# A two-block model in one program: weights and inputs as on-chip images, one weight ring, layers written out, small stages folded away

## What is computed

```python
# first block, per layer l of 2
h = rms_norm(x, attn_norm_g[l])
pa, pb, pc = split(h @ w_in[l], (1056, 768, 448))
x = x + concat([rwkv7_mixer(pa, ...), dilated_mixer(pb, ...), mla_mixer(pc, ...)]) @ w_out[l]
h = rms_norm(x, ffn_norm_g[l])
x = x + (silu(h @ w_gate[l]) * (h @ w_up[l])) @ w_down[l]          # d_ff = 2816
x = rms_norm(x, final_norm_g)                                       # after both layers
# second block, per layer i of 2; a second stream xc (256 context tokens) starts from ctx
mod  = silu(c) @ ada_w[i] + ada_b[i];  modc = silu(c_ctx) @ ada_w[i] + ada_b[i]
h, hc = modulate(rms_norm(x)), modulate(rms_norm(xc))
q, k, v = project_qkv(h);  qc, kc, vc = project_qkv(hc)
x = x + g1 * (attention(q, [kc, k], [vc, v]) @ w_o[i])              # global in layer 0, window in layer 1
x = x + g2 * peer_ffn(modulate(rms_norm(x)))                        # xc likewise, in layer 0 only
# peer_ffn: 8 heads x 16 experts of 16384 per token, u and v rows of 1024 floats gathered per expert
```

## Time and profile before

| | |
|---|---|
| median of 3 runs | 3671.6 us (3670.44 to 3678.66) |
| the profiled execution | 3673.66 us, span 3671.7 us |
| granted TensorE clock, mean | 0.907 of full speed |
| PE busy | 2794.8 us (76% of the span) |
| DVE busy | 2234.2 us (61%) |
| ACT busy | 594.1 us (16%) |
| POOL busy | 1167.0 us (32%) |
| moved by DMA | 1030.17 MB, mean 281 GB/s |

### The profile page before, as it was taken

One profiled execution on the slowest core, in us unless ns is written; L12 is line 12 of the kernel. 1 busy time (PEld: TensorE's weight loads), 2 busy tenths in 40 slices (PEclk: granted clock), 3 DMA queues, 4 the chain that ended last, 5 costly groups with the idle time before them and its releaser, 6 DMA issues. The chain is left out here.

```text
span 3671.7 us, 31943 instructions
## 1 busy us (share of the span) xinstructions
PE 2794.8 (76%) x10155; PEld 1786.7 (49%) x10155; DVE 2234.2 (61%) x5260; ACT 594.1 (16%) x1616; POOL 1167.0 (32%) x1028
## 2 busy tenths in 40 slices
PE   7884568689958777998688577777759857777776
PEld 1573445478846455886457233232227743233222
DVE  0339666666556757565577777565536277776554
ACT  1221120120001102000131111111112211111111
POOL 0000244334434432445131444444400014444442
PEclk9997789789979868999899799999979989999999
DMA  8420677559978755898553899999941239999997
GB/s 285 158 90 12 240 255 271 183 196 356 364 272 311 256 175 191 309 360 308 212 180 141 342 420 421 421 421 421 416 158 69 71 127 420 421 420 420 420 419 291
DMA packets 279599, 1030.17 MB, mean 281 GB/s; under 512 B 23498, under 2 KB 74728, under 8 KB 213504
## 3 DMA queue, kind: packets, MB, share of 16 engines
q0 software_dynamic: 147456, 805.37, 56.2%
q1 hardware_dynamic: 130464, 219.82, 17.1%
q10 hardware_dynamic: 1504, 2.87, 0.2%
HBM read 1022.16 MB, written 5.82 MB: 280 GB/s over the span
## 5 line engine op out<-in xcount | busy, mean ns | idle before, releaser
L2217 PE MATMUL ps<-w_ring,diag 128*128 128x512 f32 x1216 | 576.7, 621 | 172.9 <-ACT diag L2197 172.9
L1308 POOL DMA_INDIRECT ctx_ring<-in_peer_u,expert_now x256 | 308.9, 1207 | 928.4 <-DVE expert_now L494 415.9
L2217 PE MATMUL ps<-own,diag 128*128 128x512 f32 x832 | 406.4, 636 | 204.4 <-ACT diag L2197 204.4
L2131 DVE SCALAR_TENSOR_TENSOR w_ring<-w_ring,htok 128x1024 f32<-128x1024 f32 x304 | 372.2, 1224 | 242.1 <-DMA w_ring<-in_peer_uv,expert 241.6
L2217 PEld LDWEIGHTS ps<-w_ring,diag 128*128 128x128 f32 x1216 | 227.3, 195 | 518.5 <-ACT diag L2197 280.3
L2118 POOL DMA_INDIRECT w_ring<-in_peer_uv,expert x304 | 336.5, 1107 | 404.1 <-PE ps L2217 391.4
L2118 POOL DMA_INDIRECT own<-in_peer_uv,expert x208 | 221.7, 1066 | 705.6 <-POOLq L161 396.5
L1320 DVE SCALAR_TENSOR_TENSOR ctx_ring<-ctx_ring,h_now 128x1024 f32<-128x1024 f32 x256 | 306.7, 1224 | 120.4 <-DMA ctx_ring<-in_peer_u,expert_now 110.5
L2217 PEld LDWEIGHTS ps<-own,diag 128*128 128x128 f32 x832 | 159.8, 201 | 448.2 <-ACT diag L2197 277.3
L2131 DVE SCALAR_TENSOR_TENSOR own<-own,htok 128x1024 f32<-128x1024 f32 x208 | 254.6, 1224 | 185.8 <-DMA own<-in_peer_uv,expert 185.6
L1324 DVE SCALAR_TENSOR_TENSOR ctx_sum<-ctx_ring,weight_now,ctx_sum 128x1024 f32<-128x1024 f32 x208 | 267.0, 1284 | 126.7 <-DMA ctx_ring<-in_peer_v,expert_now 118.5
(11 more groups left out here) (419 smaller groups left out, 3774.5 us busy)
## 6 DMA issues: line engine op xcount, KB each, us to landing
w_ring<-in_ada_w SPq DMA_DIRECT2D x24, 2048.0 KB
w_ring<-in_peer_w_q SPq DMA_DIRECT2D x12, 2048.0 KB
w_ring<-in_ffn_w_gate SPq DMA_DIRECT2D x22, 1024.0 KB
w_ring<-in_ffn_w_up SPq DMA_DIRECT2D x22, 1024.0 KB
w_ring<-in_ffn_w_down SPq DMA_DIRECT2D x10, 2048.0 KB
w_ring<-in_w_qkv SPq DMA_DIRECT2D x9, 2048.0 KB
w_ring<-in_w_o SPq DMA_DIRECT2D x6, 2048.0 KB
w_ring<-in_w_in SPq DMA_DIRECT2D x6, 2048.0 KB
```

The source lines that it names most:

```text
L1308: pool.indirect_dma_start(out=m.ctx_ring[:, r % CTX_RING, :], out_offset=None, in_=expert_tables(self.d)[r // SLOTS], in_offset=bass.Indir ...
L2131: v.scalar_tensor_tensor(out=u, in0=u, scalar=1.0, in1=m.htok[:, blk, :], op0=ALU.mult, op1=ALU.mult, accum_out=b.dots[:, e:e + 1]).then_i ...
L2217: ins = pe.matmul(m.ps[:, 2 * blk + half, :], b.diag[:, e % DIAGS, :], entry(e)[:, D + half * 512:D + (half + 1) * 512], start=(k == 0), s ...
```

## The change

- Weights: the host writes each weight group as the image of its slot, `[128, n]`, one behind the other, so each load is one DMA with one contiguous run per partition (16 KB for most). One ring counts through the whole program. `peer_queries` of the context stream, and each `feed_forward`, now load the next stage's first three groups.
- Vectors, x, ctx, the peer keys and the lora matrices come from the host as they lie on the chip; the transposes for them go. The output is written feature by token and turned by the host.
- `load_constants`, both `load_inputs`, `context_keys`, `context_back` and `second_modulation` go. Their loads and the rotary angles move into `modulation`, the latent tables and keys into the second `feed_forward`, and the rest into layer 0's `peer_experts`, before expert 16 on PE and before expert 18 on VectorE.
- The first block's layers are written out; the copies at the start of `in_projection` go, and POOL's gathers no longer wait for them. The expert sums of the context stream stay on the chip.
- `peer_experts` keeps ten entries: three of its own, one in `hT`, six in the weight ring; its accumulator's copy moves into `hT`.

```diff
@@ WeightRing
-            for dst, src in self.groups[g](layer):
-                eng.dma_start(dst(self.slot(g)), src).then_inc(self.mem.w_landed[g % WSLOTS], 16)
+            n, at = self.sizes[g], self.offsets[g]
+            eng.dma_start(self.slot(g)[:, 0:n], self.images[at:at + P * n].rearrange("(p n) -> p n", p=P)
+                          ).then_inc(self.mem.w_landed[g % WSLOTS], 16)
+def rows_to_partitions(a):
+    k = a.shape[0] // P
+    return a.reshape(k, P, a.shape[1]).transpose(1, 0, 2).reshape(P, k * a.shape[1])
@@ in_projection
-            ring.load(sp, G_IN, G_MOD + WSLOTS, l)
+            sp.dma_start(m.lora[:, :, :], d.lora[l]).then_inc(s.loras, 16)
+            ring.load_to(sp, g0 + G_MOD + WSLOTS)
-            pool.wait_ge(s.experts_ready, 1)
             rows.fetch(pool, "in_projection")
-            link(v.tensor_copy(m.expert_now[:, :], one(m.ctx_expert)), s.experts_ready)
-            link(v.tensor_copy(m.vec[:, 0:VEC1_ROWS], m.vec_all[:, ds(l * VEC1_ROWS, VEC1_ROWS)]))
-            link(v.tensor_copy(m.weight_now[:, :], one(m.ctx_weight)))
-            link(v.memset(m.ctx_sum[:, :], 0.0))
@@ feed_forward
-            ring.load(sp, G_OUT + 2 + WSLOTS, G_DOWN + ND, l)
-            sp.wait_ge(m.ctx_used, 2 * SLOTS - CTX_TAIL)
-            sp.dma_start(m.kept_sum[ds(l, 1)].rearrange("o p f -> (o p) f"), m.ctx_sum[:, :]).then_inc(s.kept, 16)
-            sp.wait_ge(s.kept, 16)
+            if last:
+                latent_tables(sp, m, d, s.tables_in)      # latent, kept_k, kept_v: three DMAs
+            ring.load_to(sp, g0 + G_FIRST_END + WSLOTS)
+            if last:
+                sp.wait_ge(s.tables_in, 16 * LATENT_TABLES)
@@ first_block
-    load_inputs(nc, m, first_vectors(d), m.vec_all, d.x[0], m.xT, positions=d.positions[0])
-    ring = WeightRing(m, first_groups(d))
-    with nc.Fori(0, DEPTH) as l:
+    for l in range(DEPTH):
+        m.vec = m.vectors[:, l * VEC1_ROWS:(l + 1) * VEC1_ROWS]
         first_layer(nc, m, d, ring, l)
@@ modulation, ScalarE
+            act.dma_start(m.vectors[:, :], d.vectors).then_inc(s.vectors_in, 16)
+            act.dma_start(m.c[:, :], d.consts).then_inc(s.consts_in, 16)
+            act.dma_start(b.pos_i[:, :], d.positions[0].partition_broadcast(P)).then_inc(s.pos_in, 16)
+            act.dma_start(m.sink[:, 0, :], d.attn_sinks_2[0].partition_broadcast(P)).then_inc(s.sink_in, 16)
+            act.dma_start(m.cT[:, :, :], d.ctx_by_feature).then_inc(s.inputs_in, 16)
+            act.dma_start(m.xT[:, :, :], d.x_by_feature).then_inc(s.inputs_in, 16)
+            act.wait_ge(s.vectors_in, 16)
             act.activation(b.sig[:, :], cond, ACT.Sigmoid).then_inc(s.sig_done, 1)
...
+            act.wait_ge(s.reduced, 1)
+            act.activation(m.rope[...], b.angle[...], ACT.Sin).then_inc(s.sin_done, 1)
+            act.wait_ge(s.inputs_in, 32)
@@ modulation, PE and VectorE
+                if g == 1:
+                    pe.wait_ge(s.consts_in, 16)
+            position_angles(v, link, m, s, b)
@@ peer_queries
-            sp.dma_start(b.subk[:, :, :], d.peer_sub_keys_2[i].rearrange("s k e -> k s e")).then_inc(s.keys_in, 16)
+            sp.dma_start(b.subT[:, :, :], d.keys_by_feature[i]).then_inc(s.keys_in, 16)
             ring.load_to(sp, g0 + NG_PQ + prefetch)        # prefetch=WSLOTS for the context stream
-            pe.wait_ge(s.keys_in, 16)
-            for half in range(2):
-                ins = pe.transpose(m.ps[:, 6, half * P:(half + 1) * P], b.subk[:, half, :], m.ident)
@@ peer_experts, layer 0
+                sp.dma_start(products, m.kept_mod.rearrange("z (k p) -> k z p", p=P)).then_inc(s.products_in, 16)
+                sp.dma_start(m.cT[:, :, :], m.kept_c).then_inc(s.stream_in, 16)
+            def context_back():
+                v.wait_ge(s.products_turned, 1)
+                modulation_gains(...)                      # three small instructions
+                v.wait_ge(s.stream_in, 16)
+                for k in range(KT):
+                    v.wait_ge(s.sums_turned, k // 2 + 1)
+                    v.scalar_tensor_tensor(out=m.cT[:, k, :], in0=m.ps[:, 4 + k // 2, ...], ...).then_inc(s.context_done, 1)
             for e in range(TOTAL):
+                if between and e == CONTEXT_AT + 2:
+                    context_back()
                 dot(e)
...
+                if between and e == CONTEXT_AT:
+                    turn_context()                         # PE: 2 + 16 transposes
+                if between and e == SLOTS:
+                    pe.wait_ge(s.context_done, KT)
@@ write_out
-                        ins = pe.transpose(m.ps[:, 2 * t + j, k * P:(k + 1) * P],
-                                           m.xT[:, 4 * j + k, t * P:(t + 1) * P], m.ident)
+            sp.dma_start(d.out, m.xT[:, :, :]).then_inc(s.written, 16)
+            sp.wait_ge(s.written, 16)
```

More of the change, by code:

```diff
@@ L164, with __init__ @@
 class WeightRing:
[L167 to L173, removed]
+    def __init__(self, mem, images, sizes):
+        self.mem, self.images, self.sizes = mem, images, sizes
+        self.offsets = [sum(P * n for n in sizes[:g]) for g in range(len(sizes))]
         self.started = 0
@@ L177, in slot, with load_to @@
         return self.mem.w[:, g % WSLOTS, :]
[L179 to L181 removed]
+    def load_to(self, eng, g1):
+        for g in range(self.started, min(g1, len(self.sizes))):
             if g >= WSLOTS:
                 eng.wait_ge(self.mem.w_used, g - WSLOTS + 1)
[L184 to L190 removed]
@@ L220, in layer_rows @@
[L220 to L259, removed]
-        c = 256 * i
[L261 to L269, removed]
@@ L280, with vector_table, tokens_by_feature, lora_table @@
 VEC1_ROWS = 42
[L284 to L293, removed]
+VEC2 = dict(norm1_gain_2=0, norm2_gain_2=8, q_norm_gain_2=16, k_norm_gain_2=17, ada_b_2=18, c_2=66, c_ctx_2=74)
+VEC2_ROWS = 82
+def vector_table(a):
+    out = []
+    for l in range(DEPTH):
+        mu = np.zeros(9 * P, np.float32)
+        mu[:A_PROJ] = a["a_mu"][l]
+        for name in VEC1:
+            out.append((mu if name == "a_mu" else a[name][l].reshape(-1)).reshape(-1, P))
+    out.append(a["final_norm_g"].reshape(-1, P))
+    for i in range(DEPTH):
+        for name in VEC2:
+            out.append((a["c_2"][0] if name == "c_2" else a["c_ctx_2"] if name == "c_ctx_2" else a[name][i]).reshape(-1, P))
+    return np.concatenate(out).T
+FINAL_AT = DEPTH * VEC1_ROWS
+VEC2_AT = FINAL_AT + KT
+def tokens_by_feature(x):
+    return x.reshape(SEQ, KT, P).transpose(2, 1, 0)
+def lora_table(a):
+    t = np.zeros((DEPTH, P, 4, A_WIDTH), np.float32)
+    t[:, 0:64, 0], t[:, 64:128, 1] = a["a_decay_up"], a["a_iclr_up"]
+    t[:, :, 2], t[:, 0:32, 3] = a["a_gate_up"][:, 0:P], a["a_gate_up"][:, P:160]
+    return t
 POSITION_BUFFERS = [("pos_i", [P, SEQ], I32), ("pos", [P, SEQ], F32), ("turns", [P, 2, SEQ], F32),
@@ L1138, in _ @@
         def _(sp):
-            ring.load_to(sp, prefetch) if l is None else ring.load(sp, prefetch[0], prefetch[1], l)
+            ring.load_to(sp, group + NG_O + WSLOTS)
         if rows:
@@ L1292, in __init__ @@
         self.taken = 0
+        self.before = l * (2 * SLOTS - CTX_TAIL)
         at, self.until = 0, {}
@@ L1528, in build, with use_layer @@
+        second_block(nc, m, d, ring)
         write_out(nc, m, d)
-VEC2 = dict(norm1_gain_2=0, norm2_gain_2=8, q_norm_gain_2=16, k_norm_gain_2=17, ada_b_2=18, c_2=66, c_ctx_2=74)
+def use_layer(m, i):
+    m.mod, m.gain = m.mods[:, i, :, :], m.gains[:, i, :, :, :]
+    m.vec2 = m.vectors[:, VEC2_AT + i * VEC2_ROWS:VEC2_AT + (i + 1) * VEC2_ROWS]
 SH1, SC1, G1, SH2, SC2, G2 = (8 * i for i in range(6))
-def second_groups(d, parts):
-    sizes = dict(ada_w_2=NG_ADA, w_qkv_2=NG_QKV, w_o_2=NG_O, peer_w_q_2=NG_PQ)
-    def cols(w, layer, c):
-        return lambda l: [(view(KT, 512), columns(w, layer, c, c + 512))]
-    return [cols(d[name], i, 512 * j) for i, name in parts for j in range(sizes[name])]
```

452 lines of the change are left out of this document (178 added, 274 removed).

## The result

The changed kernel takes 3636.1 us (median of four runs, 3630.4 to 3641.3), the kernel before 3671.0 us beside it: a ratio of 0.9905, 95% interval 0.9882 to 0.9929. It is 35 us faster, where 67.5 were forecast, and the time lies 4 us above the range for eight in ten (3576 to 3632). The profiled execution took 3640.5 us, with a span of 3638.7.

A forecast was written before the change was run, and what follows sets the result against it. No engine bounds the whole (PE 76% of the span, VectorE 61%); `peer_experts`, 36% of the span, is DMA-bound. Mostly seam savings, less +16 for prefetches, sum to -67.5 us: median 3671.6 to 3604, eight-in-ten range 3576 to 3632.

The forecast's parts named there:

- The seams: Gaps between large stages, from last useful instruction to next first one; each removed stage leaves a barrier, costed seam by seam.
- start: Program start to first weight matmul: first group loaded a stage earlier, matmul at 11 instead of 20.95 us, -10 us.
- both layer seams: First layer to second, -12.0 us, and first block to second, -12.1 us, from removed waits and stages.
- the seam before `in_projection`: Last routing instruction to in_projection's product: starts at 394.1 instead of 415.64 us with weights already there, -21.5 us.
- the one between the layers of the second block: Last addition to next square: of 29.85 us only one barrier of 3.1 stays, -26.8 us.
- the end: From 3661.37 us to the span's end: 8.4 instead of 10.3 us, -1.9, bounds 0 and -5.
- The stall at expert 18: In peer_experts, new waits stall VectorE some 6 us; DMA should not run dry, at most +6 us.
- What these two prefetches cost: feed_forward's tail: three 2 MB weight loads delay gathered rows, +8 us per layer, bounds +2 and +15, +16 for two.
- Gathers beside longer runs: rwkv's late rows and each layer's groups: long weight runs need less engine time, -3 us both layers, bounds -25 and +20.
- Rival C: Long runs starve gathers in rwkv, feed_forward and in_projection: 22 groups at 5 us, 110 us lost, 3714 us; chance 0.04.
- Rival A: Prefetches give both layer seams back in full: feed_forward tails cost 2x20 instead of 16 us, 3628 us; chance 0.12.

The follow-up runs named there:

- e3: Changed kernel, 16 KB runs, but feed_forward no longer loads the next stage's first three groups; 3617.9 us, ratio 0.987.
- e7: Changed kernel, 16 KB runs, with eight instead of four landing places for gathered rows in feed_forward; 3529.4 us, ratio 0.962.
- e4: Kernel before the change, with only the feed_forward weights loaded from host images in 16 KB runs; 3699.4 us, ratio 1.010.
- e5: Changed kernel with 16 KB runs for modulation and context weights, 1 KB for all behind them; 3576.7 us, ratio 0.975.
- e6: Changed kernel with 1 KB runs beside gathered rows and no loads for the next stage in feed_forward's tail; 3570.6 us, ratio 0.974.
- e2: Changed kernel with every weight image stored for runs of 1 KB instead of 16 KB; 3581.2 us, ratio 0.977.
- e9: Changed kernel with 1 KB runs beside gathered rows and eight landing places in feed_forward; 3560.0 us, ratio 0.973.
- e8: Changed kernel with 512 B runs beside gathered rows, four landing places; 3626.2 us, ratio 0.989.

## Why the prediction was wrong

**The seams** were right: start, both layer seams, the seam before `in_projection`, the one between the layers of the second block and the end were forecast at -84.3 and measured at -87.9 us (the end alone at -3.3). Their method was to subtract a stage and keep a barrier and a norm. At the start the number was right partly by luck: I had taken 11 us from when the first weight group lands, but what the matmul waited for was the 128 KB of `vectors`, to which I had given no time of its own. In the seam between the layers, addition to square took 2.4 us instead of 8.0. Jump, copies, ring clearing and the wait for `kept_sum` all went at once, so no run tells which of them the 5.6 us were. The stall at expert 18 was nothing that shows: the first `peer_experts` took 665.9 us instead of 663.8.

**"What these two prefetches cost"** is the step that failed: +16 in the sum, +67.9 measured in the stage. It holds two errors.

1. The size. e3 shows 13.5 and 11.2 us per layer for the prefetches with 16 KB runs, against +8; by the idle tails alone it is 12.2 and 16.1, the second above the bound of +15. I had derived 4.7 us per load from 2.9 and 1.9 us per row as engine time, as if rows were short of bandwidth. They were short of places: e7 moves the same loads and has no tail.
2. The sign. I wrote that the down groups "before them, faster for the same reason, give some 4 back". e4 shows the opposite: 14.2 and 17.1 us more per layer by the long runs alone, 32 us over the program. The step took a load's engine time (5 us instead of 6) for its effect on a row.

So of the 67.9 us 24.7 are the prefetches (changed kernel less e3) and 43.2 the long runs (e3 less before): 31.2 as in e4, and 12 more that e4 doesn't have. Taken in the other order the split would differ, since with 1 KB runs the same prefetches cost the stages only 11.7 us (e5 less e6). Those 12 lie in the gate and up products, which took 165.7 and 165.8 us in e3 and 159.5 and 160.6 in e4. The changed kernel has them in layer 0 alone (166.9 and 160.9), and with eight places (e7) they are gone, 160.8 and 159.5. Whether it is the long runs of the stages ahead that bring VectorE into the stage later wasn't tried.

**"Gathers beside longer runs"**, -3, was meant for the groups of the whole layer. Outside `feed_forward` the stages did gain, 10.8 us. In `rwkv` the waits barely moved (28.8 us against 32.6), well within the 15 us that I had set as the limit. The row waits rose in other stages: in layer 0 from 16.0 to 27.6 us in `in_projection` and from 5.2 to 10.9 in `out_projection`, much the same in layer 1. What made the 10.8 us wasn't isolated, and part of it may be scatter: these stages took 775.8 to 782.9 us in the four kernels with the change and 16 KB runs, and 783.7 to 791.8 in the three without it. The kernels with 1 KB runs have 3 (e5), 7 (e2) and 14 us (e9) of it.

**Rival C** had the right mechanism, at 0.04, and the wrong extent. Its condition was right too: beside each load a row waits nearly 6 us, where it gave 5. But I charged that to 22 groups, all on the path. The waits are on the path only where VectorE's lag isn't caught up before the stage ends, and that is mainly in `feed_forward`, 43 us instead of 110: `in_projection`, from its first product to the next stage's, grew by only 0.7 and 3.6 us, though its waits rose by 12 in each layer. My argument against it, that "engine time is the same or less, and four entries in order must drain soon after", is what fails. They drain, and then the engines idle, since only four requests can stand at once. Rival A (the tail loads cost 20 us per layer) was nearer in time, 3628, but e3 puts its mechanism at 11 to 16 us per layer, with the rest of the miss elsewhere.

The Trainium skill (DMA: Bandwidth & Descriptors, section "Queues, rings and completion order") has an engine switch between queues only at the end of a packet. The runs with 16, 4 and 1 KB agree in direction: the queue with the longer runs goes ahead, in `feed_forward` (rows late by 6 us behind 16 KB runs) and at the start. The 512 B runs of e8 don't, and no run shows at what length an engine takes its turns.

## What to carry to other kernels

When a transfer's layout is improved, ask what shares its engines with it: longer runs make that load quicker (landing in 10.7 us instead of 15.8, e7 and e9) and each small request beside it later. If the small requests go through a short ring, count its places: a delay of 6 us at 1.3 us a row is five rows beside those in work; six places still fell short and eight sufficed. A DMA share that *falls* while somebody waits for DMA (0.95 to 0.82 here) points to too few requests, and what helped was depth, not fewer bytes. Rows as late beside a share of 1.04 (e8) are another case; more places weren't tried there.

## What the runs showed of the hardware that was not expected

- Between two direct loads it goes the same way. At the start, the first weight group and the constants (1867 KB) load side by side. With weight runs of 16, 4 and 1 KB the first weight matmul started at 10.0, 14.7 and 21.7 us, the constants landed in 17.6, 10.9 and 9.6 us, and the small `vectors` in 8.7, 3.0 and 2.9. With 4 and 1 KB the matmul waited for the weights; with 16 KB it waited for `vectors`, so the weights may have been there earlier (in e7, with the same loads, the first group landed at 8.85 us). Before the change the constants took 7.0.
- With the engines' share at 1.00 or above, the down products moved 401 GB/s at 16 KB runs (e7, share 1.00), 367 at 1 KB (e2, 1.02) and 352 at 512 B (e8, 1.04); rows and weights share them in somewhat different parts. The Trainium skill (DMA: Bandwidth & Descriptors, section "Specifications") puts the smallest transfer for line rate at 512 B; here a run of 512 B is not there yet.
- The profile books the 512 B runs as packets of 2 KB: 5,511 packets for 11.09 MB in the down products. Their tail (36 us) is that of 4 KB runs (37), not below that of 1 KB (22), so the number of bytes for which an engine stays with one queue may not be the run itself; or the rows are late only because the engines are full. No run here settles that.
- Four more places of 4 KB a partition were worth more (101 us on top of the change) than all the edits of the change together (35).
